# A seventh landing place for weight chunks, and the channel chunks of tiles 1 and 2 loaded before the query chunks

## What is computed

```python
mod = silu(cvec) @ w_mod + b_mod                       # 12 chunks of 512 columns: "mod" 0..11
h = rmsnorm(x, norm_attn) * (1.0 + sc_a) + sh_a
da_q, da_k, da_v, dn_q, dn_k, dn_v, dn_z, dn_b, dn_a = split(h @ w_in)   # "da" 0..2, "dn" 0..2, "z"
o_da = diff_attention(...)                             # softmax(q1 k1) - lam * softmax(q2 k2), times v
qkv = silu(short_conv(concat[dn_q, dn_k, dn_v]))       # 12 blocks of 128 channels, 5 taps
o_dn, s_f, s_b = gated_delta_chunked(both directions)
x = x + g_a * (concat[o_da, o_dn] @ w_out)             # "out" 0, 1
h = rmsnorm(x, norm_ffn) * (1.0 + sc_f) + sh_f
q = (h @ w_pq)                                         # "pq" 0..3, the query chunks
s = einsum(q, sub_keys)                                # scores against 8 heads x 2 x 128 keys
eidx, gates = product-key top 16 of 128 x 128 experts per head
coef = gates * gelu(h . expert_u[eidx])                # 128 rows of u and 128 rows of v per token
x = x + g_f * sum(coef * expert_v[eidx])
```

## Time and profile before

| what | us |
|---|---|
| median of three runs | 1314.84 |
| the profiled execution's own time | 1308.87 |
| its span | 1307.1 |
| TensorE busy (matmul) | 999.9 |
| VectorE busy | 876.1 |
| ScalarE busy | 295.0 |
| GpSimd busy | 562.6 |

### The profile page before, as it was taken

One profiled execution on the slowest core, in us unless ns is written; L12 is line 12 of the kernel. 1 busy time (PEld: TensorE's weight loads), 2 busy tenths in 40 slices (PEclk: granted clock), 3 DMA queues, 4 the chain that ended last, 5 costly groups with the idle time before them and its releaser, 6 DMA issues.

```text
span 1307.1 us, 15197 instructions
## 1 busy us (share of the span) xinstructions
PE 999.9 (77%) x5204; PEld 590.7 (45%) x5204; DVE 876.1 (67%) x2295; ACT 295.0 (23%) x760; POOL 562.6 (43%) x599
## 2 busy tenths in 40 slices
PE   7899989989899996899800354678777777776776
PEld 5756788854567784577400011223233222222322
DVE  0546349999973889627599900996779666666665
ACT  2563324621544553132000020010020000100001
POOL 0010104146577456556777677234333433333331
PEclk9899999999899997899955678799998999999999
DMA  9988349889999799999999999999999999999995
GB/s 386 362 322 323 154 153 353 332 287 407 348 409 408 273 399 405 399 401 401 409 409 410 403 406 412 389 423 421 421 422 420 421 422 421 421 421 422 421 422 234
DMA packets 96684, 492.57 MB, mean 377 GB/s; under 512 B 10720, under 2 KB 11616, under 8 KB 68192
## 3 DMA queue, kind: packets, MB, share of 16 engines
q0 software_dynamic: 83840, 404.26, 77.1%
q1 hardware_dynamic: 12768, 87.33, 16.8%
HBM read 488.93 MB, written 2.62 MB: 376 GB/s over the span
## 4 chain that ended last, share of the span: by engine, by line
DMA 28%; PE 25%; DVE 14%; POOL 7%; issue 4%; ACT 1%; POOLq 0%; DVEq 0%; ACTq 0%
PE bank L1295 25%; DMA wring<-in_euv,consts 21%; DVE big L2164 5%; POOL big L860 4%; DMA big<-in_eu,consts 2%; DVE wring L2164 2%; DMA big<-in_ev,consts 1%; DMA big<-in_eu,idx 1%; DVE W L2188 1%; DMA big<-in_euv,consts 1%; DVE extra L2164 1%; DMA extra<-in_ev,rowT 1%; POOL extra L860 1%; POOL big L849 1%; PE bank L1301 1%
## 5 line engine op out<-in xcount | busy, mean ns | idle before, releaser
L1295 PE MATMUL bank<-big,W 128*32 128x512 f32 (+1 forms) x932 | 302.1, 657 | 89.8 <-DVE W L2188 56.9
L2164 DVE CUSTOM_DVE_ANT_0 big<-big,hnow 128x1024 f32<-128x1024 f32 x226 | 270.4, 1217 | 79.1 <-DMA big<-in_euv,consts 63.8
L1295 PE MATMUL bank<-wring,W 128*128 128x512 f32 (+1 forms) x456 | 176.3, 625 | 68.4 <-DVE W L2188 67.0
L1295 PEld LDWEIGHTS bank<-big,W 128*32 128x32 f32 (+1 forms) x932 | 104.1, 156 | 256.5 <-issue 248.8
L2164 DVE CUSTOM_DVE_ANT_0 wring<-wring,hnow 128x1024 f32<-128x1024 f32 x90 | 108.9, 1219 | 112.4 <-DMA wring<-in_euv,consts 112.2
L870 POOL DMA_INDIRECT big<-in_euv,consts x113 | 107.3, 950 | 150.2 <-PE bank L1295 143.2
L860 POOL DMA_INDIRECT big<-in_ev,rowT x119 | 113.1, 950 | 67.3 <-issue 37.4
L1295 PEld LDWEIGHTS bank<-wring,W 128*128 128x128 f32 (+1 forms) x456 | 65.1, 173 | 167.6 <-issue 166.2
L870 POOL DMA_INDIRECT wring<-in_euv,consts x76 | 72.3, 952 | 139.0 <-PE bank L1295 132.8
L1295 PE MATMUL bank<-big 128*128 128x128 f32 (+1 forms) x1056 | 116.2, 266 | 8.2 <-DVE big L1925 4.3
L1295 PEld LDWEIGHTS bank<-big 128*128 128x128 f32 (+1 forms) x1056 | 106.7, 179 | 24.0 <-issue 11.1
(11 more groups left out here) (364 smaller groups left out, 1504.7 us busy)
## 6 DMA issues: line engine op xcount, KB each, us to landing
wring<-in_wch SPq DMA_DIRECT2D x23, 2048.0 KB, 11.0
big<-in_wch SPq DMA_DIRECT2D x4, 1536.0 KB, 14.0
dn_tok<-in_wch SPq DMA_DIRECT2D x4, 1536.0 KB, 11.0
tok<-in_wch SPq DMA_DIRECT2D x6, 768.0 KB, 8.0
z<-in_wch SPq DMA_DIRECT2D x6, 512.0 KB, 10.8
gate<-in_wch SPq DMA_DIRECT2D x6, 512.0 KB, 12.4
tok<-in_wch SPq DMA_DIRECT2D x4, 512.0 KB, 15.1
extra<-in_wch SPq DMA_DIRECT2D x4, 512.0 KB, 12.8
```

Of the source, the lines that this page charges most:

```text
L1295: return nc.tensor.matmul(out, lhsT, rhs, start=first, stop=last)
L2164: V.tensor_tensor_reduce(u, u, hnow[:, :], 1.0, 0.0, ALU.mult, ALU.add, coef[t % 2][:, n:n + 1]).then_inc(dot_ready, 1)
```

## The change

The list of chunks is reordered: dn.0.1, dn.1.1 and dn.2.1 come before pq.0.0, pq.1.0, pq.2.0 and pq.3.0. Their places change with it: dn.0.1 goes to ring 4, dn.1.1 to ring 0, dn.2.1 to ring 1, pq.0.0 to the new ring 6 ("seventh", rows 0 to 3 of big, after S.0.0), pq.1.0 to ring 2 (after out.0.0), pq.2.0 to ring 5 (after S.0.1), pq.3.0 to ring 3 (after out.1.0), mod.10 to ring 0, mod.11 to ring 1, and from there on rings 0 and 1 alternate the other way round. The seventh place has no semaphore of its own: it shares that of the masks. Since the query chunk now lies in the convolution's rows, `pads_again` waits for the product pq.0.0 instead of S.0.0. The loads of the sub-keys (keys_of) keep their waits, but those of pq.2.0 stand behind pq.3.0. On TensorE, channels.3.1 moves ahead of channels.4.1, channels.9.1 ahead of channels.11.1, and mod.10 moves ahead of query.2.0. The orders of the other engines are as before.

```diff
@@ -66,17 +66,17 @@
 CHUNKS = ([("mod", m, 0) for m in range(4)] + [("dn", 0, 0), ("dn", 1, 0), ("da", 0, 0), ("dn", 2, 0), ("da", 1, 0), ("da", 2, 0)]
           + [("z", 0, 0)]
           + [("mod", m, 0) for m in range(4, 10)]
-          + [("out", 0, 0), ("out", 1, 0)] + [("pq", i, 0) for i in range(2)] + [("dn", i, 1) for i in range(3)]
-          + [("pq", i, 0) for i in (2, 3)] + [("mod", 10, 0), ("mod", 11, 0)]
+          + [("out", 0, 0), ("out", 1, 0)] + [("dn", i, 1) for i in range(3)] + [("pq", i, 0) for i in range(4)]
+          + [("mod", 10, 0), ("mod", 11, 0)]
           + [token_chunk(c, 1) for c in DEFER]
           + [("out", 0, 1), ("out", 1, 1)] + [("pq", i, 1) for i in range(4)])
 CHUNK_NO = {c: n for n, c in enumerate(CHUNKS)}
 STORED = [c for c in CHUNKS if c[2] == 0]
-FIVE = CHUNK_NO["pq", 0, 0]
-AFTER = [0, 1, 3, 5, 0, 1, 3]
+FIVE = CHUNK_NO["dn", 0, 1]
+AFTER = [0, 1, 6, 2, 5, 3]
 RING_OF = ([n % 5 for n in range(FIVE + 1)] + AFTER
-           + [(n - FIVE) % 2 for n in range(FIVE + 1 + len(AFTER), len(CHUNKS))])
-PIECES = [1, 1, 2, 4, 2, 1]
+           + [(n - FIVE - len(AFTER) - 1) % 2 for n in range(FIVE + 1 + len(AFTER), len(CHUNKS))])
+PIECES = [1, 1, 2, 4, 2, 1, 1]
 BACK = [max([m for m in range(n) if RING_OF[m] == RING_OF[n]], default=None) for n in range(len(CHUNKS))]
 THIRD, FIFTH = [max(n for n in range(len(CHUNKS)) if RING_OF[n] == r) for r in (2, 4)]
 
@@ -218,9 +218,9 @@
 dn_p.0.1.5 dn_t.0.0.5 dn_p.0.0.6 dn_t.0.1.5 dn_p.0.1.6 value.0.3 dn_t.0.0.6 dn_t.0.1.6 dn_v.0.0:2 dn_o.0.0:2 mod.8:10
 dn_s.0.0 gate.0.0.0 warm.5 o_turn.0 mod_turn.9 gate.0.0.1 w_out.0.0:2 w_out_rest.0.0:2 warm.6 x_turn.1.0 dn_s.0.1
 query.0.0 query_rest.0.0 h_turn.0 key_score.0.0 channels.0.1 channels.1.1 query.1.0 query_rest.1.0 channels.2.1
-key_score.1.0 channels.4.1 c_turn.0.1 channels.3.1 channels.5.1 c_turn.1.1 channels.6.1 c_turn.2.1 channels.7.1
-c_turn.3.1 channels.8.1 c_turn.4.1 channels.10.1 channels.11.1 channels.9.1 c_turn.5.1 query.2.0 query_rest.2.0
-c_turn.6.1 c_turn.8.1 key_score.2.0 c_turn.7.1 query.3.0 query_rest.3.0 c_turn.10.1 c_turn.9.1 c_turn.11.1 mod.10:12
+key_score.1.0 channels.3.1 channels.4.1 c_turn.0.1 channels.5.1 c_turn.1.1 channels.6.1 c_turn.2.1 channels.7.1
+c_turn.3.1 channels.8.1 c_turn.4.1 channels.10.1 channels.9.1 channels.11.1 c_turn.5.1 mod.10 query.2.0 query_rest.2.0
+c_turn.6.1 c_turn.8.1 key_score.2.0 c_turn.7.1 query.3.0 query_rest.3.0 c_turn.10.1 c_turn.9.1 c_turn.11.1 mod.11
 key_score.3.0 qk_turn.2 mod_turn.11 dn_decay.2.1 expert_rows.0.0 dn_scores.2.1 token.0.1 dn_t.2.1.0 dn_p.2.1.1
 token.0.2 dn_t.2.1.1 dn_p.2.1.2 dn_t.2.1.2 dn_p.2.1.3 dn_t.2.1.3 dn_p.2.1.4 dn_t.2.1.4 dn_p.2.1.5 token.1.1:3
 qk_turn.1 dn_t.2.1.5 token.2.1 dn_decay.1.0 dn_p.2.1.6 token.3.2 token.3.1 dn_t.2.1.6 token.2.2 dn_scores.1.0 dn_w.2.1
@@ -451,6 +451,7 @@
         fourth = [tok[:, 1, :], tok[:, 2, 2 * CH:3 * CH], z[:, 1:NT, :], gate[:, 1, :]]
         fifth = [dn_tok[:, 1:NT, :], extra[:, 0:D]]
         sixth = big[:, 4 * D:8 * D]
+        seventh = big[:, 0:4 * D]
         third = [big[:, 9 * D:12 * D].rearrange("p (k c) -> p k c", c=CH), tok[:, 2, 0:2 * CH].rearrange("p (k c) -> p k c", c=CH)]
 
         def heads(ap):
@@ -579,7 +580,7 @@
 
         chunk_in = [sem(f"chunk_in{i}") for i in range(6)]
         params_in, consts_in, x_in, masks_in, kv_in, s0_in, nout_in = [
-            sem(n) for n in ("params_in", "consts_in", "x_in", "masks_in", "kv_in", "s0_in", "nout_in")]
+            sem(n) for n in ("params_in", "consts_in", "x_in", "masks_and_seventh_in", "kv_in", "s0_in", "nout_in")]
         sample_in = sem("sample_in")
         cache_out, state_out, y_out = sem("cache_out"), sem("state_out"), sem("y_out")
         product = signal("product")
@@ -645,10 +646,14 @@
             if ring == 4:
                 return ([dn_tok[:, 1 + i // 3, CH * (i % 3):CH * (i % 3) + CH] for i in range(6)]
                         + [extra[:, CH * i:CH * i + CH] for i in range(2)])
-            return [sixth[:, CH * i:CH * i + CH] for i in range(KD)]
+            if ring == 5:
+                return [sixth[:, CH * i:CH * i + CH] for i in range(KD)]
+            return [seventh[:, CH * i:CH * i + CH] for i in range(KD)]
 
         def chunk_here(*name):
             n = CHUNK_NO[name]
+            if RING_OF[n] == 6:
+                return masks_in, 32
             return chunk_in[RING_OF[n]], sum(16 * PIECES[r] for r in RING_OF[:n + 1] if r == RING_OF[n])
 
         def col(ap, n):
@@ -684,6 +689,21 @@
 
         @block.sync
         def _(sp):
+            def keys_of(i, t):
+
+                if (i, t) == (0, 0):
+                    sp.wait_ge(*product.at("modT", 9))
+                elif (i, t) == (1, 0):
+                    sp.wait_ge(*w_clear.at(0))
+                elif (i, t) == (1, 1):
+                    sp.wait_ge(*product.at("s", 3, 0))
+                elif t and i > 1:
+                    for u in (1, 2):
+                        sp.wait_ge(*product.at("s", i - 2, u))
+                else:
+                    sp.wait_ge(*product.at("s", (i - 2) % 4, 0))
+                sp.dma_start(subkeys(i, t), subk[i]).then_inc(sk_in[i % 2], 16)
+
             sp.dma_start(Q[:, :], par).then_inc(params_in, 16)
             sp.dma_start(xs[:, 0, :], x[:, 0, :]).then_inc(x_in, 16)
             sp.dma_start(K[:, :], cst).then_inc(consts_in, 16)
@@ -705,9 +725,12 @@
                 elif RING_OF[n] == 4:
                     for piece, a, b in zip(fifth, (0, 6), (6, 8)):
                         sp.dma_start(piece, wch[src, :, a:b]).then_inc(chunk_in[4], 16)
-                else:
+                elif RING_OF[n] == 5:
                     sp.wait_ge(*product.at("S", 0, 1))
                     sp.dma_start(sixth, wch[src]).then_inc(chunk_in[5], 16)
+                else:
+                    sp.wait_ge(*product.at("S", 0, 0))
+                    sp.dma_start(seventh, wch[src]).then_inc(masks_in, 16)
                 if n == 4:
                     sp.dma_start(xs[:, 1:NT, :], x[:, 1:NT, :]).then_inc(sample_in, 16)
                     sp.dma_start(wb[:, :, :], wba).then_inc(sample_in, 16)
@@ -719,21 +742,10 @@
                         sp.wait_ge(*used_up(g))
                     sp.dma_start(kTa[:, :, P:2 * P], kcT).then_inc(kv_in, 16)
                     sp.dma_start(vca, vc).then_inc(kv_in, 16)
-                if name[0] == "pq":
-
-                    _, i, t = name
-                    if (i, t) == (0, 0):
-                        sp.wait_ge(*product.at("modT", 9))
-                    elif (i, t) == (1, 0):
-                        sp.wait_ge(*w_clear.at(0))
-                    elif (i, t) == (1, 1):
-                        sp.wait_ge(*product.at("s", 3, 0))
-                    elif t and i > 1:
-                        for u in (1, 2):
-                            sp.wait_ge(*product.at("s", i - 2, u))
-                    else:
-                        sp.wait_ge(*product.at("s", (i - 2) % 4, 0))
-                    sp.dma_start(subkeys(i, t), subk[i]).then_inc(sk_in[i % 2], 16)
+                if name == ("pq", 3, 0):
+                    keys_of(2, 0)
+                if name[0] == "pq" and name[1:] != (2, 0):
+                    keys_of(*name[1:])
             sp.wait_ge(*squares.at(1, 2))
             for q in range(2):
                 sp.wait_ge(*ids_ready.at(1, 0, q))
@@ -756,7 +768,7 @@
 
             def pads_again(u):
 
-                pool.wait_ge(*product.at("S", 0, 0))
+                pool.wait_ge(*product.at("pq", 0, 0))
                 nc.gpsimd.memset(pre[:, :, 130:132], 0.0)
                 nc.gpsimd.memset(pre[:, :, 388:390], 0.0).then_inc(*pads.next(u))
 
```

## The result

The changed kernel takes 1316.76 us (median of 12 runs, 1313.34 to 1320.96), the kernel before on the same chip 1313.99 us (12 runs, 1310.28 to 1316.74): ratio 1.0030, 95% interval 1.0018 to 1.0042. It is slower, by 2.8 us between the medians and 3.9 by the ratio, which is taken over all runs; 0.9 were forecast. The profiled execution took 1316.59 us with a span of 1314.7 us, the one of before 1308.87 and 1307.1.

A forecast was written before the change was run, and what follows sets the result against it. Gathers bound the kernel from about 327 us and TensorE ends the phase before the first v gather. Terms 0 + 0.9 (mod.10) + 0 on the median 1314.84 gave 1315.7 us, called no change; range 1311.5 to 1318.8.

The forecast's parts named there:

- forecast term of 0.9: mod.10 ahead of query.2.0 on TensorE: qk_turn.2 and the first v gather come 0.9 us late, bounds 0 and 1.74.
- slower by over 0.2%: Whole kernel: the outcome slower, made of rivals B, D, the rest and 0.02 for drift; chance 0.20.
- The later chunks only swap rings 0 and 1: Transfer queue after mod.11 and da.0.1: the later chunks just exchange rings, cost 0.
- The edits costed at 0 in 140 to 262 us: Earlier query chunks, pads, gather landing places and channel block swaps: no engine waits for them, cost 0.
- Rival A: Full DMA stretch 202.5 to 237 us: the 10.2 us of moved traffic count, 3 us gained, 1311.8 us; chance 0.18.
- Rival B: TensorE before query.2.0: mod.10's chunk lands at 236, 3.2 us wait, 4.1 us in all, 1318.9 us; chance 0.14.
- Rival C: Around qk_turn.2: the 0.9 us are swallowed and nothing moves, 1314.8 us; chance 0.21.
- Rival D: TensorE's new 0.9 us idle at 256 us lowers its clock, +5 us, 1320 us; chance 0.02.

The follow-up runs named there:

- both chunks held: Changed kernel with out.0.1 and out.1.1 both started only after dot 82, halves still swapped: 1313.51 us, ratio 1.0004 to before.
- the second profile: Changed kernel run again with no edit: 1316.80 us, ratio 1.0026 to the kernel before.
- the kernel before with swapped halves: Kernel before with only rings 0 and 1 exchanged from out.0.1 on: 1316.43 us, ratio 1.0025 to before.
- late chunks back: Changed kernel with rings 0 and 1 back in their old parts from out.0.1 on: 1314.75 us, ratio 1.0014 to before.
- the version without its two costs: Changed kernel with late chunks on their old halves and mod.10 between c_turn.8.1 and key_score.2.0: 1312.42 us, ratio 0.9981 to before.
- mod.10 in the gap: Kernel before with only mod.10's matmuls moved between c_turn.8.1 and key_score.2.0: 1312.87 us, ratio 0.9987 to before.
- loads only: Changed kernel with late chunks on their old halves and mod.10 behind query.3.0 as before: 1314.16 us, ratio 0.9998 to before.

## Why the prediction was right and wrong

**The time fell in the range, but a step priced at nothing decided it.** 1316.76 lies between 1311.5 and 1318.8, and only 1.1 us above the forecast 1315.7. That closeness is luck: the forecast stood on 1314.84, the median of three runs of the kernel before, and before took 1313.99 beside the changed kernel. Against that the change costs 2.8 us (3.9 by the ratio), three to four times the forecast term of 0.9, and the case "slower by over 0.2%", to which I gave 0.20, is the one that the ratio's interval favours.

*The step that failed* is the sentence "The later chunks only swap rings 0 and 1", priced at 0 without a row. I treated the two halves as equal because both come free before their chunk is needed. They aren't equal in when they come free: dot 78 against dot 82. The swap alone costs 2.5 us, taking it back gains 2.0, and taking back only its moment gains 2.9. The rows for it were all in the trace of before: the start of both chunks at 471.92, the wait of 3.06 us that ends at 488.48 and the z gate 7 us ahead of it. I followed each moved transfer from 140 to 262 us, and not the 2 MB that the formula for the rings moves at 470.

*How 2 MB become 2.5 us and more.* The DMA engines are full here (share 1.00 from 480 to 490 us before and after), so the chunk pushes the gathers behind it back; by estimate, 2 MB at the 410 GB/s of these stretches are 5.1 us. These are the gathers of the dots in front of the z gate. VectorE's waits there are 4.2 us (0.45 + 3.75). TensorE stands 4.36 us for it. A further part is its clock, in the windows of 490 to 500 us, the kernel before first, then the changed one, then the changed one with both chunks held:

```profile
490.00:500.00 10.00, 9.87 (x36) 5.21 (x35) 9.86 (x16) 1.20 (x2) 7.56 (x9) 1.00 1.02 409
```

```profile
490.00:500.00 10.00, 8.97 (x41) 7.07 (x42) 10.00 (x18) 2.57 (x4) 6.68 (x7) 0.77 1.00 391
```

```profile
490.00:500.00 10.00, 9.91 (x35) 5.02 (x34) 6.66 (x12) 1.01 (x2) 7.55 (x9) 1.00 1.00 400
```

The mean granted clock of this window is 0.77 in the changed kernel (0.79 in the second profile, 0.66 in the kernel before with swapped halves). In finer windows it has only two levels: it falls within the stand of 4.36 us, is 0.50 (1.2 GHz) from about 488 us to shortly before 495, and is 1.00 (2.4 GHz) again from there:

```profile
488.00:490.00 2.00, 0.00 (x0) 0.00 (x0) 0.90 (x1) 0.00 (x0) 0.00 (x0) 0.50 1.02 412
496.00:498.00 2.00, 2.00 (x9) 1.12 (x8) 2.00 (x6) 0.22 (x1) 1.39 (x3) 1.00 0.97 377
```

From the z gate to the projection it is 6.1 us instead of 4.5. The loss at the projection, 6.0 us, is thus 4.4 of late z gate (490.24 - 481.57 - 4.3) and 1.6 of slower matmuls behind it. Of the 6.0, 3.4 arrive at the last gather (4.2 and 3.5 in the other two profiles that have the early transfer): at x_turn.1.1 TensorE waited 3.77 us for ScalarE before and waits 0.82 now, which takes up 3.0.

*mod.10: right in mechanism, and in size as far as the traces go.* Forecast 0.9; qk_turn.2 is 1.07 us late in the profile, and 1.06 and 1.08 in the second one and in that with both out chunks held, which is the same program up to there; with the late chunks back it is 2.4, the fall of the clock at 246 us included. For the edit alone the times give 0.5 us in the median and 2.0 by the ratio, 0 to 3.8, which doesn't settle it. key_score.2.0 at 244.8 (244.5 said), VectorE's wait at the reciprocal 1.84 us with another of 0.67 just ahead of it (2.3 said), TensorE's stand 0.57 (about 1 said), first v gather 345.0 in each of the three with the full clock (344.8 said). The stand is shorter than the delay, since TensorE too comes 0.5 us later.

*The edits costed at 0 in 140 to 262 us: right.* No wait for a chunk at 173, 189, 233 or 237; the pads are written at 182.78 - 2.24 = 180.5, no later than before; pq.2.0 and pq.3.0 leave at 173.5 and 173.9. The version with only these edits takes the time of before (0.9998).

*Rival A (traffic counts), 0.18:* not borne out. The share of the DMA engines falls by 0.14 over 34.5 us and the kernel with only this takes the same time, though a gain of up to 2 us would not be seen. The room was given to nobody who waited.

*Rival B (mod.10's chunk late), 0.14:* not in the changed kernel. With the old queue the chunk is 0.61 us late, so the earlier loads are what pays for mod.10's new place, a place that itself brings a loss.

*Rival C (nothing moves), 0.21:* wrong for this kernel; it is what the version without its two costs measures.

*Rival D (the clock), 0.02:* not where it was put: behind the new idle of 0.57 us at 259 the clock is 1.00 in both profiles of the changed kernel. But an idle of TensorE can lower the clock, at the z gate (above) and at a gap that the prediction took for safe. Of nine profiles with the 2.16 us gap ahead of key_score.2.0, five have a mean granted clock of 1.00 in 245 to 253 us and four have 0.79. The kernel before, then mod.10 moved, then mod.10 in the gap:

```profile
245.00:253.00 8.00, 8.00 (x75) 7.09 (x77) 7.24 (x37) 6.22 (x13) 1.87 (x2) 1.00 0.78 257
```

```profile
245.00:253.00 8.00, 7.48 (x52) 7.51 (x53) 3.95 (x17) 6.67 (x18) 1.88 (x2) 0.79 0.87 361
```

```profile
245.00:253.00 8.00, 8.00 (x74) 8.00 (x73) 7.26 (x30) 6.00 (x15) 1.87 (x2) 1.00 0.85 310
```

0.21 of 8 us is 1.7 us of full-speed work lost, the part that was missing in the run with only mod.10 moved (3.1 = 1.1 + 0.6 + about 1.4). The fall comes with and without mod.10 moved (the kernel before with swapped halves has it, and so has the version with the loads only). And it comes in one profile and not in another where the programs are still the same: the kernel before and that with swapped halves are, and the changed kernel and that with the late chunks back. So it belongs to the execution, and no cost of the change hangs on it. The prediction draws on the Trainium skill (TensorE: Matmul & The Clock Gate, Part 1) for the fall of an idle TensorE to its lower clock, and said that the windows showed none: at this gap one profile couldn't show it, four of nine do. In the three profiles with the gap filled the window has 1.00. Whether the 1.4 us that this placing gains hold more than the 0.7 us seen in the gathers, because the fall is rarer, stays open: three profiles are few, and the same three have a granted clock of 0.93 in 275 to 300 us, another 3.4 us at the lower level, where the two of before have 1.00. Three of the other nine have that too (late chunks back, halves swapped, loads only), so a fall less at 245 isn't shown to be a fall less in all.

What also stays open is the last 1 us between gathers 20 and 150 in the profile after. It isn't a cost of the change in every execution: in the second profile of the changed kernel the distance goes only from 3.1 to 3.3 us there, and before's own two profiles drift by 0.8.

## What to carry to other kernels

When a formula or a table deals out places, follow each transfer it deals to its start time, to the end of the program, not only near the edit: a place that comes free earlier lets a transfer go earlier, and in a stretch where the DMA engines are full that is a cost for whoever waits next. Ask of every wait for DMA on which side of the next handover it stands, and not only how long it is: 3.4 us behind the z gate in the kernel before, 3.4 us in front of it with only the halves swapped, and the kernel is 2.5 us slower. What the wait behind the gate itself costs wasn't measured. One wait more in the transfer queue can then be a gain (here 2.9 us), and a step that must move is best tried in a gap that its engine already has (here 1.4 us faster than before, where the place ahead of query.2.0 cost 0.5 to 2.0).

## What the runs showed of the hardware

TensorE's granted clock after a stand of some microseconds isn't the same in each execution: after 2.16 us it fell in four of nine profiles, after the stands of 4.36, 2.99 and 3.56 us in front of the turned rows (o_turn.1) in all three that had one, and at the stands of 3.66 to 3.83 us in front of x_turn.1.1 in all nine that had one. In windows of 2 us it then reads 0.50, half the full clock. And single profiles of one kernel differ by 3.2 us of 1310 (1308.87 and 1312.1); over the twelve profiles up to 2.8 us are already present at mod.8, before the first place at which the times of the programs differ (141.76 to 144.54 us). A cause that is read off a pair of profiles needs that offset taken out first.
